# Two transformer blocks on one core: raw weight buffers handed out by need, and the order at the start of a pair of panels

## The reference, cut to what matters

```python
mod = jax.nn.silu(c) @ w_ada + b_ada            # one row: 2048 x 6144
shift, scale, gate = jnp.split(mod, 3, axis=-1)
h = rmsnorm_2(x, pre_g) * (1.0 + scale[:, None]) + shift[:, None]
q, k, v, gate_a, u, gate_p = jnp.split(h @ w_in, SPLIT_POINTS, axis=-1)
y_a = windowed_gqa(q, k, v, rel_table, sink) * jax.nn.silu(gate_a)
y_p = multiscale_pool(u, w_pool_grp, pool_scale) * jax.nn.silu(gate_p)
g_a, g_p = jnp.split(jax.nn.sigmoid(h @ w_merge + b_merge), 2, axis=-1)
merged = g_a * (y_a @ w_br_attn) + g_p * (y_p @ w_br_pool)
return x + gate[:, None] * rmsnorm_2(merged @ w_out, post_g)
```

## Time and profile before

| | |
|---|---|
| runs shown | 2172.28, 2174.02, 2177.65 us (median 2174.02) |
| profiled execution | 2175.93 us, span 2174.1 us |
| mean granted TensorE clock | 0.993 |
| busy | PE 2085.0 us (96%), DVE 1681.1 (77%), ACT 1173.4 (54%), POOL 74.2 (3%) |
| instructions | PE 9334, DVE 1839, ACT 1519 |
| moved by DMA | 453.75 MB, mean 209 GB/s |

### The profile page before, as it was taken

The page is one execution under the profiler, slowest core; times in us unless marked ns, Lnnn a source line. Parts: engine busy times, 40 slices in busy tenths (PEclk is TensorE's granted clock), DMA queues, the critical chain, the costliest instruction groups (busy, mean ns, idle before and its releaser), DMA issues.

```text
span 2174.1 us, 25372 instructions
## 1 busy us (share of the span) xinstructions
PE 2085.0 (96%) x9334; PEld 1700.7 (78%) x9334; DVE 1681.1 (77%) x1839; ACT 1173.4 (54%) x1519; POOL 74.2 (3%) x94
## 2 busy tenths in 40 slices
PE   9999999899999999999999999999899999899998
PEld 7887877778887777787787877877677787778786
DVE  6777777777765778898898888887687767888875
ACT  6655556755554565555455554555655554554453
POOL 1000000000000000000000000000400000000000
PEclk9999999999999999999999999999999999999999
DMA  9444546465444447676567766675455556669753
GB/s 332 155 155 169 174 159 228 167 227 208 155 155 155 155 155 276 240 281 254 213 222 269 278 217 237 233 254 197 135 182 175 174 184 218 227 242 348 232 203 107
DMA packets 218955, 453.75 MB, mean 209 GB/s; under 512 B 14400, under 2 KB 16592, under 8 KB 218704
## 3 DMA queue, kind: packets, MB, share of 16 engines
q1 hardware_dynamic: 212928, 432.07, 56.5%
q0 software_dynamic: 5616, 19.94, 2.8%
q10 hardware_dynamic: 288, 0.13, 0.0%
HBM read 447.88 MB, written 4.19 MB: 208 GB/s over the span
## 4 chain that ended last, share of the span: by engine, by line
PE 57%; DVE 19%; issue 11%; DMA 8%; ACT 5%; POOL 0%; DVEq 0%; ACTq 0%; SPq 0%; POOLq 0%
PE ps L1023 17%; PE ps L1025 17%; PE ps L1024 17%; DVE wlo L2241 8%; DVE raw L2257 3%; DMA raw<-in_w_down_dram 3%; DMA raw<-in_w_up_dram 2%; ACT whi L1535 2%; PE ps L615 1%; DMA raw<-in_w_merge_dram 1%; DMA raw<-in_w_o_dram 1%; DVE FR L1907 1%; DVE FR L1643 1%; DMA raw<-in_w_gate_dram 1%; PE ps L746 1%
## 5 line engine op out<-in xcount | busy, mean ns | idle before, releaser
L2241 DVE TENSOR_TENSOR wlo<-raw,whi 128x1024 fp32r<-128x1024 f32 x832 | 1005.4, 1221 | 307.0 <-ACT whi L1535 300.7
L1535 ACT ACTIVATE whi<-raw 128x1024 fp32r<-128x1024 f32 x840 | 879.9, 1056 | 622.1 <-PE ps L1025 363.1
L1023 PE MATMUL ps<-whi,ah 128*128 128x512 f32 x1618 | 646.5, 400 | 20.2 <-ACT side L1130 12.4
L1025 PE MATMUL ps<-whi,al 128*128 128x512 f32 x1618 | 632.8, 391 | 0.0
L1024 PE MATMUL ps<-wlo,ah 128*128 128x512 f32 x1618 | 631.8, 390 | 0.0
L1023 PEld LDWEIGHTS ps<-whi,ah 128*128 128x128 f32 x1618 | 304.9, 188 | 91.2 <-ACT side L1130 16.2
L1025 PEld LDWEIGHTS ps<-whi,al 128*128 128x128 f32 x1618 | 304.8, 188 | 65.3
L1023 PE MATMUL ps<-whi,bh 128*128 128x512 f32 x862 | 343.4, 398 | 12.0 <-ACT side L1130 9.9
L1024 PEld LDWEIGHTS ps<-wlo,ah 128*128 128x128 f32 x1618 | 305.3, 189 | 61.2 <-issue 0.2
L1025 PE MATMUL ps<-whi,bl 128*128 128x512 f32 x862 | 337.6, 392 | 0.0
L1024 PE MATMUL ps<-wlo,bh 128*128 128x512 f32 x862 | 337.4, 391 | 0.0
(11 more groups left out here) (235 smaller groups left out, 1355.3 us busy)
## 6 DMA issues: line engine op xcount, KB each, us to landing
raw<-in_w_in_dram SPq DMA_DIRECT2D x168, 512.0 KB, 5.7
raw<-in_w_ada_dram SPq DMA_DIRECT2D x96, 512.0 KB, 8.0
raw<-in_w_gate_dram SPq DMA_DIRECT2D x88, 512.0 KB, 7.4
raw<-in_w_up_dram SPq DMA_DIRECT2D x88, 512.0 KB, 6.0
raw<-in_w_down_dram SPq DMA_DIRECT2D x88, 512.0 KB, 7.0
raw<-in_w_merge_dram SPq DMA_DIRECT2D x64, 512.0 KB, 8.0
raw<-in_w_o_dram SPq DMA_DIRECT2D x32, 512.0 KB, 7.1
raw<-in_w_xk_dram SPq DMA_DIRECT2D x32, 512.0 KB, 6.5
```

The source lines that it names most:

```text
L1023: e.matmul(o, xh[:, k, tokens], wh, start=first, stop=False, skip_group_check=more)
L1025: ins = e.matmul(o, xl[:, k, tokens], wh, start=False, skip_group_check=more, stop=kk == 1 and (st.end or st.form in READ))
L1535: done(e.activation(whi[:, n % HALVES, :], raw[:, item % RAWS, :], ACT.Copy), "hi")
L2241: done(e.tensor_tensor(wlo[:, n % HALVES, :], src, whi[:, n % HALVES, :].bitcast(F32), ALU.subtract), "lo")
```

## The change

Four edits. (1) The two orders M3, M5 become M5, M3 (entry 0 and entry 1). (2) The M5 sum is tied to the entry two ahead of M5 (entry -2), the M6 sum to the entry after M3 (entry 2); the M7 and M4 sums stay. ScalarE's copy of M5 stands in M3's step, still behind the `whi` of entry 4. (3) The places of raw weights come from a table: items are loaded in the order of their first use, and each takes the place whose item has its last use earliest. (4) The items of w_ada, which have 1024 columns as before, are tied one by one to single entries: in an up pair to entries 13 to 16, in a down pair to 13 to 17, in a merge pair to 13 to 18, in a branch panel to its last two. None falls to entry 0 or 1 any more. The diff, cut:

```diff
+    def _add_ada(self, todo):
+        if todo:
+            self.ada_before[len(self.entries)] = [len(self.items)]
+            self.items.append(("ada", *todo.pop(0)))
...
         for c in range(len(panel.rows)):
             for hf in range(2):
+                if c == 1 and panel.kind in ("ba", "bp"):
+                    self._add_ada(self._late)
                 self._entry(self._item(p, c, hf))
-            if c == 1 and panel.kind in ("ba", "bp"):
-                self._load_ada(self._late, 1)
...
+        product("M5", b12, b11, start=True, job=False)
         product("M3", b22, start=True, job=False)
-        product("M5", b12, b11, start=True, job=False)
...
-        for c in range(1, chunks):
-            for hf in range(2):
-                normal(s, c, hf)
-            if self.panels[s].kind in ("u", "d") and c > (1 if self.panels[s].kind == "u" else 0):
-                self._load_ada(self._early, 1)
-            elif self.panels[s].kind == "m":
-                self._load_ada(self._late, 1)
+        todo = {"u": self._early, "d": self._early, "m": self._late}.get(self.panels[s].kind, [])
+        for i, (c, hf) in enumerate((c, hf) for c in range(1, chunks) for hf in range(2)):
+            if i < {"d": 5, "m": 6}.get(self.panels[s].kind, 4):
+                self._add_ada(todo)
+            normal(s, c, hf)
...
+        for form, n in (("M5", at["M5"] - 2), ("M6", at["M3"] + 1), ("M7", at["M1"] + 2),
+                        ("M4", max(at["M2"], at["M6"]) + 1)):
+            self.sums_before[n] = at[form]
...
+    def _loads(self):
...
+        for n, entry in enumerate(self.entries):
+            used(entry.item, (n, 2))
+            for item in self.ada_before.get(n, ()):
+                used(item, (n, 0))
+            if n in self.sums_before:
+                added = self.entries[self.sums_before[n]]
+                for item in (added.item, added.add):
+                    used(item, (n, 1))
+        self.loads = sorted(range(len(self.items)), key=lambda i: first[i])
+        self.place, self.nth_load, self.before = {}, {}, {}
+        holds, loaded = [None] * RAWS, [0] * RAWS
+        for item in self.loads:
+            at = min(range(RAWS), key=lambda r: (-1, 0) if holds[r] is None else last[holds[r]])
...
             for i, st in enumerate(stream.steps):
-                if st.snap and st.snap[0] != "v":
+                if st.snap and st.snap[0] in ("s1", "s3"):
                     snapshot(*st.snap)
                 make(st.made)
+                if st.form == "M3":
+                    snapshot("s5", role[st.p][1])
...
             def load(i):
-                slot, kind = i % RAWS, stream.items[i][0]
-                if i >= RAWS:
-                    wait_taken(i - RAWS)
+                if stream.before[i] is not None:
+                    wait_taken(stream.before[i])
...
-            for i in range(8, len(stream.items)):
+            for i in stream.loads[8:]:
                 load(i)
```

More of the change, by code:

```diff
@@ L243, in __init__ @@
         self.pool_halves = range(0)
-        self._ada, self._done, self._set, self.sums = [], 0, 1, 0
-        self._early = [(g, k) for g in range(2) for k in range(16)]
-        self._late = [(2, k) for k in range(16)]
+        self._done, self._set, self.sums = 0, 1, 0
+        self.sums_before = {}
+        self._early = [(g, k, hf) for g in range(2) for k in range(16) for hf in range(2)]
+        self._late = [(2, k, hf) for k in range(16) for hf in range(2)]
         p, used = 0, [0, 0]
@@ L258, in __init__ @@
             self._set, p = sets[-1], p + len(group)
-        assert not self._early and not self._late and not self._ada
+        assert not self._early and not self._late
         self.total = len(self.entries)
@@ L376, in _places, with used @@
         self.free = {what: last[before[what]] if what in before else 0 for what in last}
+    def _loads(self):
+        first, last = {}, {}
+        def used(item, when):
+            first[item] = min(first.get(item, when), when)
+            last[item] = max(last.get(item, when), when)
+        for n, entry in enumerate(self.entries):
[11 more added lines that the diff above has]
+            at = min(range(RAWS), key=lambda r: (-1, 0) if holds[r] is None else last[holds[r]])
+            assert holds[at] is None or last[holds[at]] < first[item]
+            loaded[at] += 1
+            self.place[item], self.nth_load[item], self.before[item] = at, loaded[at], holds[at]
+            holds[at] = item
     def lo_count(self, n):
@@ L430, in build_program, with place, loaded @@
         panels, index, role = stream.panels, stream.index, stream.role
+        def place(item):
+            return raw[:, stream.place[item], :]
+        def loaded(item):
+            return s[f"raw{stream.place[item]}"], 16 * stream.nth_load[item]
         def bank_of(p, t):
@@ L1531, in make @@
                     else:
-                        e.wait_ge(s[f"raw{item % RAWS}"], 16 * (item // RAWS + 1))
+                        e.wait_ge(*loaded(item))
                     if n >= HALVES:
                         e.wait_ge(s["half"], n - HALVES + 1)
-                    done(e.activation(whi[:, n % HALVES, :], raw[:, item % RAWS, :], ACT.Copy),
-                         "hi")
+                    done(e.activation(whi[:, n % HALVES, :], place(item), ACT.Copy), "hi")
             e.wait_ge(s["mhalf"], 1)
@@ L2250, in sum_weights @@
                 assert nth == count["t_sum"] + 1
-                for loaded in (item, add):
-                    e.wait_ge(s[f"raw{loaded % RAWS}"], 16 * (loaded // RAWS + 1))
+                for one in (item, add):
+                    e.wait_ge(*loaded(one))
                 if count["lo"]:
@@ L2314, in low_parts @@
                     made[0] += 1
-                    src = raw[:, stream.entries[n].item % RAWS, :]
+                    src = place(stream.entries[n].item)
                     e.wait_ge(s["hi"], n + 1)
@@ L2448, in sync_program @@
                 e.dma_start(XT[j], xT_v[:, 4 * j:4 * j + 4, :]).then_inc(s[f"xt{j}"], 16)
-                load(2 * j)
-                load(2 * j + 1)
-            for i in range(8, len(stream.items)):
+                for i in stream.loads[2 * j:2 * j + 2]:
+                    load(i)
+            for i in stream.loads[8:]:
                 load(i)
```

35 lines of the change are left out of this document (10 added, 25 removed).

## The result

| | before | after |
|---|---|---|
| median of the runs shown | 2174.0 us | 2144.4 us |
| lowest to highest | 2172.3 to 2177.7 | 2141.9 to 2144.8 |
| profiled execution, span | 2175.9, 2174.1 | 2141.9, 2140.1 |
| mean granted TensorE clock | 0.993 | 0.993 |

The ratio is 0.9859, with a 95% interval of 0.9842 to 0.9876: 29.6 us faster (forecast 37, range 14 to 50).

The account below looks back on a forecast made before the run. TensorE, with 57% of the chain, was taken to set the time, held up by late `wlo`s and M5 copies; `wlo` waits 26 + copies 8 + clock 4 = 38 us gained, forecast 2137 us, 2124 to 2160 for 8 in 10.

Parts of the forecast that it names:

- (a) Counts: Whole kernel: no loads, sums, adds, roundings, copies or matmuls added or taken away; time can only come from waits.
- (b) to (d), the `wlo` waits: TensorE's waits for VectorE's `wlo`, mostly at M3 and M5: place table, moved sums and single w_ada adds together gain 26 us.
- the reserve of (b): Raw-weight loads: with the table none gets less than 8.15 us of TensorE's work, 770 of 808 over 10.
- the slower case: VectorE stands behind the load of b11; if loads pile up to 16 us, 17 pairs lose 4.3 each: 2183, chance 0.06.
- (b), the rule: Loads share 16 DMA engines, so earlier ones may land later, up to 11.4 us: time 2147, chance 0.1 inside the forecast.
- (c), what else stands behind the sum: M5 sum moved past two `wlo`s and evacuations: only wlo -2 and -1 queue behind it, wanted 5 us later.
- (e) The copies: Waits for ScalarE's copy of M5: 8 us taken of 10, from merge pairs 5.8, w_o, w_xk and w_xo pairs 3.4.
- (f) The clock: TensorE clock drops behind copy waits of 2 us and more: three waits shrink, 4 us taken, 5.1 at best.
- The sum: Whole kernel: 26 + 8 + 4 = 38 us gained, giving 2138 from the profiled execution, 2136 from the median; 2137 said.
- the rivals: Given back in the middle 2156 (0.18), slower 2183 (0.06), nothing 2174 (0.06), more than forecast 2122 (in the forecast's range).
- given back in the middle of the pairs: Rival: half the `wlo` waits (13 us) return at M7, M4 or entry 12, copies 5: 2156, chance 0.18.
- The signs: Pairs of 43 to 44 us, `wlo` waits under 6, load waits at most 1, copy waits 13 to 20, 3 or 4 clock drops.

## Why the prediction was right, and where not

**(a) Counts.** Right: 9334, 1839 and 1519 instructions on the three engines in both kernels (PE, DVE, ACT).

**(b) to (d), the `wlo` waits: 26 us forecast, 24.1 measured.** With the 0.27 us hidden per wait, 32.1 us became 5.8 + 8 x 0.27 = 8.0. The size is right and so are the places (25 us at M3 and M5, 0.8 left). The forecast left the three parts in one sum; the runs divide it. The table alone brings 23.7 us; the single adds bring 3.3 alone and 9.3 in company; the new order brings nothing and, alone, costs 91.6. The reason is the reserve of (b): where the load of b11 has no reserve, everything behind its sum waits. That it needs the table so badly was underestimated: the slower case was priced on a trip that rises ("if the new loads pile up to 16 us"), at 2183; without the table it is the reserve that falls, to 4.08 us and less, and the time is 2251.5. The price of that case was summed wrongly too: the 26 us of `wlo` waits are part of the 38, so 73 stood against 38 and not against 38 + 26, which makes 2209.

**(b), the rule.** Loads issued earlier did not land later. Against 5.7 and 8.0 us in the earlier trace rows they land in 4.5 and 4.5. The Trainium skill, "DMA: Bandwidth & Descriptors", section "Issuing engines are not separate DMA queues", says in my words that transfers share the 16 DMA engines and interleave. That an earlier load then lands later was my own step. The traces agree with the sharing in another way. In the kernel before, a load issued with none of the others under way lands in 3.9 us (median), with two under way in 5.7, with four in 7.3, with seven in 10.5; 438 of the 816 loads had four or more ahead of them. After, the trips grow in the same way (3.7, 4.7 and 6.4 us with none, two and four), but only 80 loads had four or more ahead. In the ring, one step that gave its place back released several loads together that had stood behind it in order: 106 loads were issued within 0.5 us of the one before, in the kernel after none. With the table alone the median trips are 4.7 and 4.8 us, without the table 7.1 and 6.9 (w_ada and w_merge).

**(c), what else stands behind the sum.** This step failed: "behind it are queued wlo -2 and -1, which TensorE wants 5 us later". The prediction named the evacuations that the sum passes and did not ask for them one by one, and three places pay. Ahead of the first pair an evacuation is queued behind the sum and its load had not landed: 3.7 us of wait instead of 1.9 and a clock drop follow, 4.2 us. It is shown by moving that one sum, which brings back 3.3 us at this place. In the second pair the sum (106.31) stands ahead of the softmax operations L1823 and L1827, for which ScalarE waits 4.03 us where it waited 2.90, and the copy behind them comes 1.1 us later:

```profile
109.48 0.40 ACT L1257 ACTIVATE FR<-FR,Z 128x128 f32<-128x128 f32 x1 [4.03 <-DVE Z L1827]
```

In the old order, with table and singles, TensorE waits 1.9 us for this copy, as before. Ahead of the window pair it is the sum of 3.41 us beside GpSimd, which costs TensorE 1.3.

**(e) The copies: 8 forecast, 4.3 measured.** 29.2 us became 20.3 + 17 x 0.27 = 24.9. The prediction took all 17 waits for the copy of M5; four of them, with 3.2 us, are for other copies, and of these the one at M4 of the first w_xk pair grew by 0.6 us. In the three merge pairs the mechanism was right: waits of 1.9 us each became 0.25, 0.7 and 0.7, together 4.2 us instead of 5.8, since the copy ends 4.4 us after the step in the first and 4.9 in the others, and not near 4.1. In the pairs of w_o, w_xk and w_xo the term was mis-sized: 3.4 forecast, and the wait fell by 1.1 us in the w_o pair and by 0.8 in the w_xo pair, and stayed at 4.0 in the w_xk pair. In the second pair it rose from 1.9 to 3.1 us, by the sum ahead of the softmax. In all these pairs it is still an operation of VectorE that ScalarE waits for ahead of the copy (in the w_xk pair L1776, 4.6 us), and the copy stands behind the rounding of entry 4 besides. What this rounding costs is shown: with the copy ahead of it seven of the waits go, the copy waits fall to 13.2 us in 10, and the time by 7.3.

**(f) The clock: 4 forecast, 0 measured.** Five drops are gone, among them those behind the copy waits at 765 and 1946, as expected, but new ones came at 46.7, 1531 and 1685, and the one near 412 lasts twice as long. Seven drops of 3.4 us at half speed before and five with 23.9 us in all after come to the same 11.9 us lost. A clock drop was counted as if it hung on its wait alone; it moved to other places when the waits moved. The five drops behind copy waits before stand behind waits of 1.9 to 4.0 us, so "2 us and more" was not quite so either. With the old order, table and singles 6.8 us are lost instead of 11.9. These are figures of one profile each, and why a drop comes in one place and not in another stays open.

**The sum.** By profiles 24.1 + 4.3 + 0 = 28.4, and other waits (transposes, the start, the attention stages) with 5.6 make the 34.0. Of these 5.6 the transposes of the w_ada sums (L788 before, L821 after) have 2.5. From the forecast's side: 38 less 1.9 (`wlo`), 3.7 (copies) and 4 (clock), and 5.6 more, is 34.0. The other 4.4 us down to 29.6 are the two profiled executions' distances from their medians; the forecast allowed for the first, 1.9, alone. The forecast's own range held the time, and none of the rivals came. Nothing was given back in the middle of the pairs: two gate/up pairs are longer than before (45.6 and 45.3 us), but by the transposes of the w_ada sums, which stood at the end of other pairs before. They took 6.8 us of TensorE's time there, 2.1 of it one wait, and take 4.3 us now.

**The signs.** As forecast: gate/up, down and merge pairs of 42 to 44 us but for those two, the first gate/up pair (44.6) and the first merge pair (50.1), `wlo` waits under 6 us, and no `wlo` wait at entries 9 to 13 that was not there before. Not as forecast: the first M5 sum waits 2.42 us for its load, the copy waits end at 20.3 us, with short ones left in the merge pairs, and there are five drops of the clock.

## What to carry to other kernels

When a ring of buffers holds items of different lifetimes, give out the places by last use and load in order of first use, before anything else is reordered: it cost no instruction and brought four fifths of the gain. An operation that waits for a load may be moved ahead in an in-order queue only after its load has the reserve for it in every place, the first one of the program included, and after asking in each place what else stands behind it and who waits for that. Test the parts of a joint change singly and by leaving each out; here one of the three parts was harmless only thanks to another, and a simpler gain, the copy ahead of a rounding, was left unused, though it can be had in either order.

## What the runs showed of the hardware beyond that

- The landing time of a 512 KB load goes with the number of loads that are under way when it is issued: in the kernel before 3.9 us (median) with none and 10.5 with seven. So the medians are 8.0 us (w_ada before), 7.1 (without the table) and 4.5 (after), for the same loads and the same bytes, while the DMA share within the pairs was higher in the last.
- A sum of two raw buffers on VectorE takes 1.23 us alone and took 3.41 beside a GpSimd subtraction of the same size (1545.72 to 1548.29 in the kernel after).
- A wait of equal length brings a clock drop in one place and none in another. Matmuls behind two copy waits in the kernel before: behind 1.93 us the next ones keep 0.39 us, behind 1.91 us they take 0.63 from the fourth on.

```profile
1898.82 0.50 PE L1023 MATMUL ps<-whi,ah 128*128 128x512 f32 x1 [1.93 <-ACT side L1130]
...
1899.62 0.40 PE L1023 MATMUL ps<-whi,ah 128*128 128x512 f32 x1
```
```profile
1945.70 0.50 PE L1023 MATMUL ps<-whi,ah 128*128 128x512 f32 x1 [1.91 <-ACT side L1130]
...
1946.60 0.63 PE L1023 MATMUL ps<-whi,ah 128*128 128x512 f32 x1
```
